# A hybrid decoder layer on one core: gate units, value slab, convolution norm and chunk 0 put in another order

## What is computed

```python
proj = hn @ w_in          # u_glu(1024) q(512) k(512) v(1024) r(1024) a_low(16) gate_c(1024) gate_g(1024)
# convolution branch
u = a * sigmoid(b)                                   # a, b: the halves of u_glu
y = depthwise_conv(u, width 31) + conv_db
yn = (y - mean(y)) * rsqrt(var(y) + EPS) * ln_g + ln_b
conv_out = silu(yn) @ w_pw
# gated linear attention branch, state carried along the tokens
log_a = log_sigmoid(a_low @ w_gate_up + b_gate_up) / 16
b = cumsum(log_a)                                    # within a chunk
o = (q * exp(b)) @ S + (masked q k^T exp(b_t - b_s)) @ v
S = exp(b_last) * S + (k * exp(b_last - b))^T @ v
gla_out = (rms_norm(o) * silu(r)) @ w_gla_out
# both, then the experts
h = x + (sigmoid(gate_c) * conv_out + sigmoid(gate_g) * gla_out) @ w_out
out = h + hier_moe(rms_norm(h))                      # 32 experts, top 2 of one group of 8
```

## Time and profile before

| | us |
|---|---|
| median of 3 runs | 1825.35 |
| lowest and highest run | 1823.4, 1826.05 |
| the profiled execution, whole | 1825.37 |
| its span, first to last instruction | 1823.7 |

### The profile page before, as it was taken

How to read it: one execution, slowest core, us unless ns; L and a number is a source line. 1 busy time by engine, 2 the same in 40 slices (tenths; PEclk the granted TensorE clock), 3 DMA queues, 4 the chain that set the end, 5 groups by cost and what they waited for, 6 DMA issues and landing times.

```text
span 1823.7 us, 24424 instructions
## 1 busy us (share of the span) xinstructions
PE 1707.9 (94%) x8996; PEld 1491.7 (82%) x8996; DVE 1233.5 (68%) x1991; ACT 912.6 (50%) x1094; POOL 230.0 (13%) x260
## 2 busy tenths in 40 slices
PE   7999989999899999989999996999999999999991
PEld 7999978777899999958998885788888888887771
DVE  5243889962666565653445555998989888888873
ACT  5361121114443333323434333888877877787863
POOL 3100101000000000001000122211111112232210
PEclk9999999999999999989999997999999999999995
DMA  5301222231134322163534327899999999999955
GB/s 193 132 36 59 82 82 101 93 106 41 60 92 142 115 87 87 43 197 102 177 127 173 105 91 269 330 359 376 361 378 389 385 390 389 381 374 380 353 211 196
DMA packets 102813, 366.70 MB, mean 201 GB/s; under 512 B 14413, under 2 KB 57633, under 8 KB 88912
## 3 DMA queue, kind: packets, MB, share of 16 engines
q1 hardware_dynamic: 79824, 308.49, 45.6%
q0 software_dynamic: 22704, 57.12, 9.7%
q10 hardware_dynamic: 208, 0.08, 0.0%
HBM read 324.87 MB, written 61.22 MB: 212 GB/s over the span
## 4 chain that ended last, share of the span: by engine, by line
PE 84%; DMA 7%; DVE 4%; issue 2%; ACT 2%; DVEq 1%; ACTq 0%; SPq 0%; POOLq 0%
PE bank L998 81%; DMA wraw_down<-in_w_expert_down 4%; DMA wraw_gate<-in_w_expert_gate 1%; PE bank L1409 1%; PE bank L1430 1%; DVE fbuf L2478 1%; PE bank L1330 0%; PE bank L1201 0%; ACT wH_down L1498 0%; DMA stage<-xn_scr,kdT 0%; PE bank L1007 0%; DVE wL_gate L1907 0%; DMA uo<-in_x_prompt 0%; DVE attn L2145 0%; DMA h_scr<-ybuf,kdT 0%
## 5 line engine op out<-in xcount | busy, mean ns | idle before, releaser
L1907 DVE TENSOR_TENSOR wL_down<-wraw_down,wH_down 128x2048 fp32r<-128x2048 f32 x72 | 161.8, 2289 | 57.7 <-ACT wH_down L1498 57.7
L1907 DVE TENSOR_TENSOR wL_up<-wraw_up,wH_up 128x2048 fp32r<-128x2048 f32 x72 | 161.5, 2285 | 16.5 <-ACT wH_up L1498 16.5
L1907 DVE TENSOR_TENSOR wL_gate<-wraw_gate,wH_gate 128x2048 fp32r<-128x2048 f32 x72 | 161.6, 2286 | 5.8 <-ACT wH_gate L1498 5.7
L1498 ACT ACTIVATE wH_up<-wraw_up 128x2048 fp32r<-128x2048 f32 x72 | 134.1, 1911 | 60.6 <-DMA wraw_up<-in_w_expert_up 45.5
L1498 ACT ACTIVATE stage<-bank 128x512 f32<-128x512 f32 (+4 forms) x63 | 33.4, 546 | 259.3 <-PE bank L998 259.3
L2021 DVE SCALAR_TENSOR_TENSOR ybuf<-uo,gwork,ybuf 128x1024 f32<-128x1024 f32 x120 | 153.6, 1280 | 6.1 <-issue 6.1
L1498 ACT ACTIVATE wH_down<-wraw_down 128x2048 fp32r<-128x2048 f32 x72 | 133.8, 1911 | 13.2 <-DMA wraw_down<-in_w_expert_down 13.1
L998 PE MATMUL bank<-nTH,gateH 128*128 128x352 f32 x384 | 132.5, 345 | 5.3 <-DVE gateL L1907 5.3
L1498 ACT ACTIVATE wH_gate<-wraw_gate 128x2048 fp32r<-128x2048 f32 x72 | 134.2, 1922 | 2.0 <-DMA wraw_gate<-in_w_expert_gate 2.0
L998 PE MATMUL bank<-nTH,slabH 128*128 128x352 f32 x384 | 126.8, 330 | 2.1 <-DVE nTL L1907 1.8
L998 PE MATMUL bank<-nTL,slabH 128*128 128x352 f32 x384 | 124.9, 325 | 0.0
(11 more groups left out here) (310 smaller groups left out, 4291.3 us busy)
## 6 DMA issues: line engine op xcount, KB each, us to landing
wraw_gate<-in_w_expert_gate SPq DMA_DIRECT2D x36, 2048.0 KB, 16.2
wraw_up<-in_w_expert_up SPq DMA_DIRECT2D x36, 2048.0 KB, 15.5
wraw_down<-in_w_expert_down SPq DMA_DIRECT2D x36, 2048.0 KB, 17.6
slab_raw<-in_w_in SPq DMA_DIRECT2D x7, 2048.0 KB, 8.4
gate_scr<-stage POOLq DMA_DIRECT2D x16, 528.0 KB, 3.5
vr_scr<-stage POOLq DMA_DIRECT2D x32, 256.0 KB, 2.3
gate_raw<-in_w_in SPq DMA_DIRECT2D x16, 512.0 KB, 8.7
vrbuf<-vr_scr SPq DMA_DIRECT2D x16, 512.0 KB, 6.7
```

The source lines that it names most:

```text
L1498: return act.activation(out, in_, func, **kw)
L1907: return dve.tensor_tensor(out, x, y, op)
```

## The change

Four edits.

1. The convolution gate units get the odd numbers and the low-rank ones the even. The wait for alow's copy moves from ahead of all eight units to ahead of each low-rank unit.
2. ScalarE rounds part c of slab 4 before it evicts key unit c, where it did so behind the eviction of unit c + 1. VectorE's stretches of rounds ahead of the low parts of slabs 4 and 5 are cut at round 6 in place of round 7.
3. LN_JOB is (27, 29, 31) in place of (27, 30, 33).
4. Preparing chunk 0 is taken apart. ScalarE rounds the first two gate weight tiles behind tile 33 and takes the level exponentials behind tile 34, so ahead of tile 35's eviction; only the last two exponentials stay behind the tiles. VectorE takes the level products before it waits for the end of the tiles, and the key difference behind that wait. PE waits ahead of the gate blocks for 32 of the 36 tiles, and for all 36 behind the three gate blocks.

```diff
         NPROJ = 1 + H + 3 * CC
 
 
-        Z_JOB, B_JOB = (1, 3, 5, 7), (2, 4, 6, 8)
+        Z_JOB, B_JOB = (2, 4, 6, 8), (1, 3, 5, 7)
         N_A, N_K = 1 + H + CC, 1 + H + 2 * CC
         NU = 3 * CC
 
-        LN_JOB = (27, 30, 33)
+        LN_JOB = (27, 29, 31)
         NEWC_JOB = (3, 6, 9)
         assert sorted(Z_JOB + B_JOB) == list(range(1, 1 + H + CC))
         VRJ = 4 * NT
...
 
             pe.wait_ge(low_made, 5)
             project(0, lambda out, j: by_token(out[:, 0:BLK], lambda k: walH[:, k, :], lambda k: walL[:, k, :], third(j)))
-            pe.wait_ge(taken[0], 1)
             pe.wait_ge(early_loaded, 16 * 5)
             for n in range(1, 1 + H + CC):
                 if n in Z_JOB:
                     h = Z_JOB.index(n)
+                    pe.wait_ge(taken[0], 1)
                     project(n, lambda out, j: mm(out[0:P, 0:BLK], wup[:, h * DK:(h + 1) * DK], alow[:, third(j)],
                                                  True, True))
                 else:
...
 
             pe.wait_ge(centred_normed, 5)
             pe.wait_ge(squared_std, 6)
-            pe.wait_ge(staged, 2 * NU + VRJ)
+            pe.wait_ge(staged, 2 * NU + VRJ - 4)
 
 
             def gate_block(c, b, k, j, parts=range(KC)):
...
                 for j in range(3):
                     gate_block(c, b, 0, j)
                 pe.wait_ge(prep_made, c + 1)
+                pe.wait_ge(staged, 2 * NU + VRJ)
                 lv = lev.rearrange("p l (h t) -> p l h t", h=H)
                 for l in range(LV + 2):
                     x = (LV + 2) * b + l
...
 
             for c in range(CC):
                 n = N_K + c
+                slab_high(4, c)
                 act.wait_ge(proj_ready, n + 1)
                 for j in range(3):
                     take_unit(1, 3 * c + j, bk[3 * (n % 2) + j])
-                if c >= 1:
-                    slab_high(4, c - 1)
-            slab_high(4, 3)
             INV = 1.0 / GATE_NORM
 
-            def factors(c, b, gate):
-
+            def level_factors(c, gate):
                 for l in range(LV):
                     act.wait_ge(diff_made, c * (LV + 1) + (l + 1))
                     f(lev[:, l, :], lev[:, l, :], ACT.Exp, scale=INV).then_inc(exp_made, 1)
                     if l in (2, 5):
                         gate(l // 3)
+
+            def last_factors(c, b):
                 act.wait_ge(diff_made, c * (LV + 1) + (LV + 1))
                 f(ebuf[:, :, :], qkb[b][:, 2, :, :], ACT.Exp, scale=INV).then_inc(exp_made, 1)
                 f(kdT[:, :, :], kdT[:, :, :], ACT.Exp, scale=INV).then_inc(exp_made, 1)
...
                         v = ybuf[:, c, j * BLK:(j + 1) * BLK]
                         last = f(v, v, ACT.Silu, scale=par[:, 24 + c:25 + c], bias=par[:, 28 + c:29 + c])
                     last.then_inc(y_ready, 1)
-            for k in range(2):
-                gate_high(0, 0, k, 16)
-            factors(0, 0, lambda j: None)
+                if m == LN_JOB[2] + 2:
+                    for k in range(2):
+                        gate_high(0, 0, k, 16)
+                if m == LN_JOB[2] + 3:
+                    level_factors(0, lambda j: None)
+            last_factors(0, 0)
 
             for b in range(3):
                 act.wait_ge(spilled[b], 16 * ((2 * NU + VRJ) // 3))
...
                 f(rstd4, ss4, ACT.Sqrt, scale=1.0 / DV, bias=eps_t).then_inc(o_rms, 1)
                 gate_out(c, 1, 0)
                 if nxt:
-                    factors(c + 1, 1 - b, lambda j: gate_out(c, 1, 1 + j))
+                    level_factors(c + 1, lambda j: gate_out(c, 1, 1 + j))
+                    last_factors(c + 1, 1 - b)
                     gate_high(c + 1, 1 - b, 1, landed)
                 else:
                     for j in range(1, 3):
...
                         dve.scalar_tensor_tensor(ysamp[:, c], us[:, c, :, bass.ds(w, NS)], tap, ysamp[:, c],
                                                  ALU.mult, ALU.add)
 
-            for s, (w0, w1) in zip((4, 5, 6, 7, None), ((1, 7), (7, 13), (13, 21), (21, 28), (28, CW))):
+            for s, (w0, w1) in zip((4, 5, 6, 7, None), ((1, 6), (6, 13), (13, 21), (21, 28), (28, CW))):
                 taps(w0, w1)
                 for part in range(4):
                     if s is not None:
...
                 v = x.rearrange("p h (n z) -> p (h n) z", z=2 * m) if n_t == P else x
                 return v[..., 0:m], v[..., m:2 * m], v[..., m - 1:m]
 
-            def prepare(c, b, loaded, first=False):
-
+            def level_diffs(b, loaded):
                 dve.wait_ge(chunk_loaded[b], loaded)
-                q, k, B = (qkb[b][:, w, :, :] for w in range(3))
+                B = qkb[b][:, 2, :, :]
                 for l in range(LV):
                     m = 64 >> l
                     le, ri = lev_halves(l, m)
...
                     mid = bm.broadcast_to([P, H * P // (2 * m), m])
                     tt(ri, br_, mid, ALU.subtract)
                     tt(le, mid, bl, ALU.subtract).then_inc(diff_made, 1)
-                if first:
-                    dve.wait_ge(slab_done, 8)
-                    dve.wait_ge(const_ready, 4)
-                    dve.memset(state[:, :, :], 0.0)
-                    dve.drain().then_inc(s_made, 1)
+
+            def key_diffs(b):
+                B = qkb[b][:, 2, :, :]
                 tt(kdT[:, :, :], B[:, :, P - 1:P].broadcast_to([P, H, P]), B, ALU.subtract).then_inc(diff_made, 1)
+
+            def level_products(c, b):
+                q, k = qkb[b][:, 0, :, :], qkb[b][:, 1, :, :]
                 for l in range(LV):
                     m = 64 >> l
                     le, ri = lev_halves(l, m)
                     dve.wait_ge(exp_made, c * (LV + 2) + (l + 1))
                     tt(ri, ri, halves(q, m)[1], ALU.mult)
                     tt(le, le, halves(k, m)[0], ALU.mult)
+
+            def last_products(c, b):
+                q, k = qkb[b][:, 0, :, :], qkb[b][:, 1, :, :]
                 dve.wait_ge(exp_made, c * (LV + 2) + (LV + 2))
                 tt(qe[:, :, :], q, ebuf[:, :, :], ALU.mult)
                 tt(kdT[:, :, :], kdT[:, :, :], k, ALU.mult).then_inc(prep_made, 1)
+
+            def prepare(c, b, loaded):
+                level_diffs(b, loaded)
+                key_diffs(b)
+                level_products(c, b)
+                last_products(c, b)
 
             def chunk(c, b, i, t0, nxt):
                 for l in range(LV + 2):
...
                 tt(qe[:, :, 0:R], q, ebuf[:, :, 0:R], ALU.mult)
                 tt(kdT[:, :, 0:R], kdT[:, :, 0:R], k, ALU.mult).then_inc(prep_made, 1)
 
-            prepare(0, 0, 48, first=True)
+            level_diffs(0, 48)
+            level_products(0, 0)
+            dve.wait_ge(slab_done, 8)
+            dve.wait_ge(const_ready, 4)
+            key_diffs(0)
+            dve.memset(state[:, :, :], 0.0)
+            dve.drain().then_inc(s_made, 1)
+            last_products(0, 0)
             with dve.Fori(0, NCH // 2 - 1) as i:
                 for b in range(2):
                     chunk(dve.snap(i * 2 + b), b, i, bass.ds(i * 256 + b * P, P), i * 48 + 48 * (b + 1))
```

## The result

The changed kernel takes 1812.0 us (median of four runs, 1810.2 to 1812.3) against 1824.4 us for the kernel before, measured beside it (1823.4 to 1826.1): a ratio of 0.9927, interval 0.9915 to 0.9939. The profiled execution shown here took 1812.27 us, its span is 1810.6; before it was 1825.4 and 1823.7.

What follows compares the result with a forecast made beforehand. The matmul engine PE, 84% of the chain, was taken to bound the kernel. Savings of 2.2 + 5.7 + 7.4 = 15.3 us from 1825.4 gave 1810.1, rounded to 1810.0 us, range 1804.5 to 1815.5.

Steps and rivals of the forecast that it cites:

- Part 1: Eight gate units, convolution first: 2.7 us won, some 0.5 us of new wait, so -2.2 us.
- only one thing is late next: Behind the reordered gate units, only VectorE's split of slab 2's part 1 would be late, some 0.5 us.
- The wait for slabL: At the next stage's second unit PE waits some 0.5 us for slab 2's part 1, too short to touch the clock.
- Part 2: Key-to-value border, slab 4 split early: 3.3 us of stop and 2.4 us of slow clock won, -5.7 us.
- The stop that I expected to remain: Before the first value tile PE still stands 1.4 us for the last key evictions, with the clock staying up.
- the seventh round: VectorE's tap round moved to stand before the split of slab 5, costed at nothing.
- Part 3: Early norm and chunk 0 prepared ahead: levels start 7.4 us earlier, 5.1 of stop and 2.3 of slow clock.
- The ring through ScalarE: Chunk 0's preparation through ScalarE and VectorE frees bank 0 for the third gate block with 0.5 us to spare.
- rival A: Border stop drops the clock (2.4 us) or a late ScalarE stops the third gate block; about 1812.5, chance 0.13.
- the rule that spoke against this edit: ScalarE table switches cost 2.66 us, so group by set; by that figure the sum is 0.6 us smaller.
- D: Expert stage: earlier start puts weight loads into a worse step with the gathers, 25 us slower, 1835; chance 0.03.
- E: Expert stage: the nine slow blocks fall back to 17.75 us, 6.9 us less, 1803; chance 0.04.

Runs made afterwards that it cites:

- p1_only: Kernel before with only the convolution gate units put ahead of the low-rank ones and alow's wait moved into those; 1822.9 us, ratio 0.9982.
- p2_only: Kernel before with only slab 4 rounded ahead of the key evictions and five tap rounds in front; 1820.7 us, ratio 0.9968.
- swap_last: Changed kernel with the last two gate units exchanged, so low-rank units stand at places 2, 4, 6, 7; 1818.4 us, ratio 0.9955.
- no_drain: Changed kernel with the drain behind the last low-rank unit replaced by a signal from the next stage's first matmul; single time 1812.4 us.
- bank3: Changed kernel with value tiles begun in bank 3, so the first doesn't wait for the last three key evictions; 1808.2 us, ratio 0.9899.
- pause_mid: Changed kernel with one more drain, behind the second of the four low-rank units; single time 1814.2 us.
- norm_back: Changed kernel with the norm again at tiles 27, 30, 33 and gateH and the level exponentials behind the value loop; 1821.5 us, ratio 0.9977.
- late_exps: Changed kernel with only chunk 0's seven level exponentials put back behind the value loop, norm still early; 1812.0 us, ratio 0.9922.
- p3_only: Changed kernel with the gate unit order and the slab 4 rounding put back, keeping early norm and chunk 0 preparation; 1818.2 us, ratio 0.9954.

## Why the prediction was right, and where it was off

The forecast (1810.0, range 1804.5 to 1815.5) holds the 1812.0, and the mechanisms are those that were written down, but for one fall of the clock that the working left out. One figure of the range has no working: the text adds nothing up to 1807.5, from which the lower bound is taken. The 1812.0 lies on the other side of the forecast, so nothing hangs on it. Point by point:

**Part 1, forecast -2.2, measured -1.4** (-1.3 in p1_only). The eight units are 3.0 us shorter, 2.7 were forecast: the stop and the slow clock at 86 to 92 us are gone. What failed is the sentence that only one thing is late next. The prediction moved a thin unit next to the drain and costed the drain at its own 0.3 us; by the earlier trace rows the clock had fallen behind a short stop followed by thin matmuls, and I did not ask where the new order puts such a pair. Undisturbed, the next stretch takes 94.23 us with a border stop of 1.26 (p2_only; swap_last has 242.94 - 148.71 = 94.23 as well), with the fall 95.82: it costs 1.6 us. The wait for slabL, forecast at 0.5 us, is real but hidden by the slow clock, so the sign named for it, a stop 11.5 us behind the last thin unit, is missing in the trace after; it is there once the clock stays up (idle for 0.58 us in no_drain, 0.29 in bank3, 0.28 in pause_mid). Set against that wait, the fall costs the kernel only about 1.0 us: the difference between 162.46 and 161.44 in no_drain.

**Part 2, forecast -5.7, measured -5.85** (3.44 and 2.41 in p2_only). The 3.44 is firm; the 2.41 is measured against the slow stretch of one execution of the kernel before, and against that of p1_only it would be 1.46. The stop that I expected to remain, 1.4 us behind the evictions, is 1.26, and the clock stays at 1.00 behind it. In the trace after, VectorE is through slab 4 long ahead of it and on with its tap rounds, and has no wait; the seventh round cost nothing:

```profile
224.94 4.62 DVE L1911 TENSOR_TENSOR slabL<-slab_raw,slabH 128x1024 fp32r<-128x1024 f32 x4
229.78 1.29 DVE L2025 SCALAR_TENSOR_TENSOR ybuf<-uo,gwork,ybuf 128x1024 f32<-128x1024 f32 x1 [0.21 <-issue]
```

**Part 3, forecast -7.4, measured -7.2** (the rest of the third stretch, 222.92 - 218.19 = 4.73, and 2.43). The ring through ScalarE, from which rival A took its case, closes with more room than I gave it. ScalarE after:

```profile
448.57 1.28 ACT L1499 ACT_TABLE_LOAD   x1
449.87 4.12 ACT L1499 ACTIVATE gwork<-gwork 128x512 f32<-128x512 f32 x7
454.00 1.28 ACT L1499 ACT_TABLE_LOAD   x1
455.30 0.59 ACT L1499 ACTIVATE stage<-bank 32x512 f32<-32x512 f32 x1
455.90 1.28 ACT L1499 ACT_TABLE_LOAD   x1
458.65 0.63 ACT L1499 ACTIVATE ebuf<-qkbuf 128x512 f32<-128x512 f32 x1 [1.46 <-DVE kdT L1911]
459.19 0.62 ACT L1499 ACTIVATE kdT<-kdT 128x512 f32<-128x512 f32 x1
459.83 0.55 ACT L1499 ACTIVATE stage<-bank,par 128x352 f32<-128x352 f32 x1
```

Bank 0 is free at 460.4, and the third gate block wants it 7.8 us behind 454.07, at 461.9: 1.5 us to spare, where the forecast had 0.5. Half of the difference is the seven exponentials, 4.12 us for the 4.66 of the working, which had read as their own time one that VectorE's differences helped to set. On the rule that spoke against this edit: each of the three loads takes 1.28 us; behind the first two the next activation starts 0.02 us later (448.57 + 1.28 = 449.85, then 449.87; 454.00 + 1.28 = 455.28, then 455.30), behind the third ScalarE waits for VectorE. The second and third start within 0.02 us of the end of the activation ahead of them. The 2.66 us a switch of the Trainium skill (ScalarE: Activation LUTs, What ACT_TABLE_LOAD costs) is not what this place pays; going by the row was right.

**Behind the levels.** The forecast added nothing there. Up to the experts' tail that holds: SP issues the same gate-weight load at 1510.33 where it was 1524.52, 14.2 us earlier, and another at 1694.84 where it was 1708.94, 14.1.

```profile
1510.33 0.33 SPq L468 DMA_DIRECT2D wraw_gate<-in_w_expert_gate  x1
...
1528.08 0.33 SPq L468 DMA_DIRECT2D wraw_gate<-in_w_expert_gate  x1
...
1694.84 0.34 SPq L468 DMA_DIRECT2D wraw_gate<-in_w_expert_gate  x1
```

The nine blocks paced by transfers take (1694.84 - 1528.08) / 9 = 18.53 us each, 18.52 before: neither D nor E. In the last 115 us one microsecond is lost, 14.1 to 13.1. The rest behind the levels differs by up to 4 us between executions (1343.5 to 1347.5, above), so where this microsecond went isn't settled.

Of the miss of 2.2 us (15.3 to 13.1), then, 1.1 is the clock's fall (1.6, less the wait of 0.5 that it hides), 0.6 the later start of this execution, and 0.8 came behind the levels (13.9 to 13.1); the rest, 0.3 us to the good, is what the other terms differ by in sum.

## What to carry to other kernels

When units are put in another order, look at what now stands next to each drain and each wait, not only at the stop that goes: a thin unit came to stand ahead of a 0.27 us drain, and in most executions the clock fell there and cost 1.6 us. Write out the ring of engines behind a gain with times, and then put back one half of a joint edit at a time: here the half without the early norm made a loss, because a bank's eviction stood behind the exponentials on ScalarE. Read a group's time as its own only if nothing paces it: the seven exponentials took 4.66, 4.12 and 3.76 us. And before an order is broken up, see what the alternation hides: two thin units side by side cost a stop of 6.1 us.

## What the runs showed of the hardware

The granted clock can fall to its lower level (0.50, that is 1.2 GHz) behind a stop of 0.22 to 0.27 us, if a thin unit (six matmuls on 16 partitions, 2.04 us) stands right ahead of it. It did so at six of the eight such places seen: behind the last thin unit in the changed kernel twice, p1_only, norm_back and late_exps, and in the middle in pause_mid. It did not in bank3 and at the end of pause_mid. The five falls at the last unit had the next stage starting at 139.70 to 140.06 us, the two that stayed up at 139.17 and 141.18, so when the stop comes may matter as much as what it stands beside; that wasn't tried apart. With the stop of 1.23 us ahead of a thin unit it fell each time (before, p2_only, p3_only). Thin units without a stop beside them never dropped it (39 of them), nor did stops of 1.26 or 1.27 us between full matmuls (eight executions), one of 1.35 us (late_exps), or the same drain with a full unit ahead (before, p2_only, p3_only, swap_last). Stops of 4.69 and 5.30 us did each time, and one of 3.68 us too (norm_back, 0.50 at 472 to 474 us). Beside the stop itself, the first 24 matmuls behind it then took between 1.3 us (norm_back, behind 5.30: 5.24 us for 3.91) and 2.6 us (p3_only, behind 4.69: 8.23 us for 5.65) more than in the changed kernel: the same stop doesn't always cost the same.
